# Products of constants that nobody reads, in TensorE's waits from the last logits to the first gate product

## The reference

```python
def _hmoe(x, w_rg, b_rg, w_re, b_re, w1, w3, w2):
    xt = x.reshape(B * T, D)
    lg = (xt @ w_rg + b_rg)                       # 4 groups
    g = jnp.argmax(lg, axis=-1)
    le = (xt @ w_re + b_re).reshape(-1, 4, 4)     # 4 experts in each group
    le_g = jnp.take_along_axis(le, g[:, None, None], axis=1)[:, 0]
    top_v, top_i = lax.top_k(le_g, 2)
    wts = softmax(top_v) * softmax(lg)[g]
    gate = ...                                    # 16 wide, two entries a row
    a = jnp.einsum('nd,edf->nef', xt, w1)         # gate products
    u = jnp.einsum('nd,edf->nef', xt, w3)         # up products
    hdn = jax.nn.silu(a) * u * gate[..., None]
    return jnp.einsum('nef,efd->nd', hdn, w2)     # down products
```

## Time and profile before

| | |
|---|---|
| runs of the kernel before | 1141.06, 1141.35, 1142.93 us; median 1141.35 us |
| profiled execution | span 1140.6 us; the page gives no other time for it |
| TensorE busy | 1031.9 us, 90% |
| VectorE, ScalarE, GpSimd busy | 544.0, 274.0, 211.2 us |
| chain that ended last | TensorE 83%, DMA 8%, VectorE 5% |
| moved by DMA | 150.10 MB, mean 132 GB/s |

### The profile page before, as it was taken

One profiled execution on the slowest core, in us unless ns is written; L12 is line 12 of the kernel. 1 busy time (PEld: TensorE's weight loads), 2 busy tenths in 40 slices (PEclk: granted clock), 3 DMA queues, 4 the chain that ended last, 5 costly groups with the idle time before them and its releaser, 6 DMA issues.

```text
span 1140.6 us, 17296 instructions
## 1 busy us (share of the span) xinstructions
PE 1031.9 (90%) x6808; PEld 615.6 (54%) x6808; DVE 544.0 (48%) x987; ACT 274.0 (24%) x557; POOL 211.2 (19%) x202
## 2 busy tenths in 40 slices
PE   7999999979999987999999999983589989899856
PEld 4666666645656544665666666552345454455322
DVE  1541033354555547577765866746234333332137
ACT  1552112221222223333333333220111111111113
POOL 0000000000111123345534533400100000000056
PEclk9999999989999989999999999995699999899978
DMA  9120202020000064101001001159399986957756
GB/s 379 60 74 1 74 1 74 1 78 1 1 0 1 1 222 174 47 20 37 20 19 37 20 19 37 48 195 422 113 363 355 331 312 208 372 193 235 256 207 258
DMA packets 30475, 150.10 MB, mean 132 GB/s; under 512 B 5602, under 2 KB 6050, under 8 KB 21322
## 3 DMA queue, kind: packets, MB, share of 16 engines
q1 hardware_dynamic: 24730, 125.96, 29.9%
q0 software_dynamic: 5248, 18.94, 4.8%
q10 hardware_dynamic: 432, 4.35, 1.0%
HBM read 317.31 MB, written 23.82 MB: 299 GB/s over the span
## 4 chain that ended last, share of the span: by engine, by line
PE 83%; DMA 8%; DVE 5%; issue 2%; SPq 1%; ACT 0%; POOL 0%; DVEq 0%; POOLq 0%; ACTq 0%
PE psum L1712 18%; PE psum L779 10%; PE psum L1763 10%; PE psum L792 8%; PE psum L1385 5%; PE psum L1351 5%; PE psum L1374 4%; PE psum L820 4%; DMA x_cm<-in_w_up 3%; PE psum L1397 2%; PE psum L1730 1%; DMA hg_q<-in_w_down 1%; PE psum L754 1%; PE psum L1336 1%; DMA weight_slots<-in_w_gate 1%
## 5 line engine op out<-in xcount | busy, mean ns | idle before, releaser
L1712 PE MATMUL psum<-x_cm,weight_slots 128*128 128x344 f32 x720 | 209.0, 453 | 0.0
L1712 PEld LDWEIGHTS psum<-x_cm,weight_slots 128*128 128x128 f32 x720 | 136.6, 190 | 71.9 <-issue 1.1
L1763 PE MATMUL psum<-weight_slots,x_cm 128*128 128x512 f32 x256 | 113.6, 597 | 0.0
L1351 PE MATMUL psum<-conv_qk,scratch 128*32 128x512 f32 x320 | 75.7, 617 | 10.8 <-issue 7.2
L1374 PE MATMUL psum<-weight_slots,scratch 128*32 128x256 f32 x1280 | 77.4, 396 | 8.1 <-DMA weight_slots<-in_w_gate 4.3
L1385 PE MATMUL psum<-conv_qk,scratch 128*32 128x256 f32 x640 | 74.3, 386 | 5.5 <-DMA x_cm<-in_w_up 5.4
L1763 PEld LDWEIGHTS psum<-weight_slots,x_cm 128*128 128x128 f32 x256 | 47.9, 192 | 54.2 <-issue 54.2
L1351 PE MATMUL psum<-hg_q,scratch 128*32 128x512 f32 x320 | 75.7, 617 | 0.0
L1385 PE MATMUL psum<-hg_decay,scratch 128*32 128x256 f32 x320 | 74.1, 386 | 0.0
L1385 PE MATMUL psum<-x_cm,scratch 128*32 128x256 f32 x320 | 74.1, 386 | 0.0
L820 PEld LDWEIGHTS psum<-scratch 128*128 128x128 f32 x448 | 58.7, 194 | 24.4 <-issue 22.7
(11 more groups left out here) (388 smaller groups left out, 1649.4 us busy)
## 6 DMA issues: line engine op xcount, KB each, us to landing
weight_slots<-in_w_gate SPq DMA_DIRECT2D x80, 1024.0 KB
conv_qk<-in_w_up SPq DMA_DIRECT2D x40, 1024.0 KB
conv_qk<-in_w_down SPq DMA_DIRECT2D x40, 1024.0 KB
hg_q<-in_w_down SPq DMA_DIRECT2D x40, 1024.0 KB
hg_decay<-in_w_up SPq DMA_DIRECT2D x20, 1024.0 KB
x_cm<-in_w_up SPq DMA_DIRECT2D x20, 1024.0 KB
weight_slots<-in_w_in SPq DMA_DIRECT2D x6, 2048.0 KB, 8.2
y_slots<-scratch SPq DMA_DIRECT2D x10, 512.0 KB, 8.5
```

The source lines that it names most:

```text
L1351: m = mm(PS[lane, 5 + half, :], hidT[:, k, lane], w_down[q][:, k, half * 512:(half + 1) * 512], start=(k == 0), stop=(k == 1))
L1712: i = mm(PS[0:m, idx % 4, 0:PIECE], lhs_of(k), xT[:, k, n * PIECE:(n + 1) * PIECE], start=(k == 0), stop=(k == KD - 1))
L1763: i = mm(PS[:, bank, :], xT[:, k, c * P:(c + 1) * P], w_slot(g)[:, k, :], start=(k == 0), stop=(k == KD - 1))
```

## The change

A helper `fill(n)` issues n products of the identity with the first 512 columns of the constants, into bank 3. It is called eight times with 34 products in all. Nothing reads bank 3 between there and the up products, which begin with `start=True` and overwrite it. No wait is added or removed. Nothing else of the program changes, but lines behind the helper have moved: 745 to 750, 754 to 759, 896 and 897 to 905 and 906, 1322 to 1332, 1326 to 1337, 1336 to 1347, 1374 to 1387; the fills are line 741.

```diff
--- before.py
+++ after.py
@@ -735,6 +735,11 @@
         pe.wait_ge(s.hg_k_ready, H)
         pe.wait_ge(s.hq_silu, H)
 
+        def fill(n):
+
+            for _ in range(n):
+                mm(PS[:, 3, :], ident, cst[:, 0:512], start=True, stop=True)
+
         def turn_x1(c):
 
             r = x_rows(c)
@@ -888,14 +893,18 @@
         pe.wait_ge(s.hgs_ready, NCH)
         route(NCH - 3)
         turn_x1(NCH - 2)
+        fill(1)
         route(NCH - 2)
+        fill(2)
         turn_x1(NCH - 1)
+        fill(2)
         route(NCH - 1)
+        fill(8)
 
         pe.wait_ge(s.esum_ready, 1)
         mm(PS[:, 6, 0:NTT * NE], const("before"), esum.rearrange("p e i -> p (e i)"), start=True, stop=True)
         mm(PS[:, 7, 0:NTT * NE], ones, esum.rearrange("p e i -> p (e i)"), start=True, stop=True).then_inc(s.ranked, 1)
-        tensor_moe(pe)
+        tensor_moe(pe, fill)
 
     def scalar_rest(act, link, tell):
         A = nc.scalar.activation
@@ -1316,10 +1325,12 @@
             out_dma(sp, t["out_y"][c * P:c * P + r], pair_of[c][0:r, 0])
         sp.wait_ge(s.outputs, 16 * outs[0])
 
-    def tensor_moe(pe):
+    def tensor_moe(pe, fill):
         mm = nc.tensor.matmul
+        fill(2)
         pe.wait_ge(s.tile_column, 2)
         mm(PS[0:1, 5, 0:TILES], tile_col, ident[:, 0:TILES], start=True, stop=True).then_inc(s.tile_row, 1)
+        fill(12)
         pe.wait_ge(s.onehots, 1)
         for q in range(2 * NTT):
             half = 64 * (q % 2)
@@ -1351,7 +1362,9 @@
                         m = mm(PS[lane, 5 + half, :], hidT[:, k, lane], w_down[q][:, k, half * 512:(half + 1) * 512], start=(k == 0), stop=(k == 1))
             m.then_inc(s.down_done, 1)
 
+        fill(6)
         turn_x(0, 0)
+        fill(1)
 
         def turn_hid(n):
 
```

## The result

The change makes the kernel faster. In 18 runs of each, the median went from 1143.23 to 1135.93 us; the ratio of the changed kernel to the one before is 0.9922, with a 95% interval of 0.9905 to 0.994, so 0.6 to 0.95% are won. The medians lie 7.3 us apart (a ratio of 0.9936); 0.9922 of 1143.23 would be 8.9 us. The forecast was 7.6 of 1141.35 us, a ratio of 0.9933. The profiled execution of the changed kernel took 1135.78 us, with a span of 1133.9: 1.9 us of a run lie outside its span.

The account below looks back on a forecast made before the run. TensorE, busy 90%, was taken as the bound, its real products from 769 to 820 mostly at half clock; gains of 7.98 less 0.35 gave 7.6 us off 1141.35, so 1133.7, range 1131.2 to 1138.4.

Parts of the forecast that it names:

- last transposes: Transposes ahead of the last router products: from 1.94 to 1.06 us at the full clock, 0.88 gained.
- last router products: Router products of the last row chunk: from 3.60 to 1.86 us at the full clock, 1.74 gained.
- slot products: Products of line 1326 before the gather: 4.07 us, about half at the full clock, 2.0 gained (ends 1.0 and 2.1).
- gather transposes: Transposes of the first gather: from 1.97 to 1.06 us at the full clock, 0.91 gained.
- first gate products: Gate products of the first tile: from 5.51 to 3.66 us at the full clock, 1.85 gained.
- The late start of 0.35: Two fills behind the last transposes: 1.72 us in a wait of 1.36, so 0.35 us late.
- The count products: Lines 896 and 897: from 1.33 us to an assumed 0.73 at the full clock, 0.6 gained (ends 0.3 and 0.7).
- "Hidden" groups: Groups of fills shorter than their waits, costing nothing, such as 8 fills of 6.9 us in 7.48, 12 of 10.3 in 11.64.
- The first rival: Clock falls at 768.5 all the same and fills bring it back: net gain 4.1 us, 1137.3; chance 0.24.
- The loop: Stretch from 820 to 1087, where the clock falls in four places, 1.9 us each; allowed plus or minus 2.5 us.
- the second rival: Four more clock falls in the loop cancel the gain: 1141.3; chance 0.10, shared with a hold-up elsewhere.
- The slower rival: Fills never win the clock, cost 1.72 us each and stand in the way: 27 us, 1168.6; chance 0.04.

Follow-up runs that it names:

- the tail: The changed kernel with 15 more fills behind the last down products, in the wait for the gather of the results; ratio to the kernel before 0.992.
- one fill for two: The changed kernel with one fill in place of two on either side of the last transposes, plus 15 fills behind the last down products; ratio to the kernel before 0.9938.

## Why the prediction was right

- **The clock held from the first fill on, and the products were cut as the rows said.** The forecast per term and what it measured, in us: last transposes 0.88 and 0.90; last router products 1.74 and 1.74; the counts 2.28 nearer in all for 2.27 forecast; slot products 2.0 and 1.90; gather transposes 0.91 and 0.82; first gate products 1.85 and 1.85.
- **The late start of 0.35** lay elsewhere than forecast, and it is luck that the sum is the same. The pair ahead of the last transposes was put at nothing, because VectorE would not have let them start sooner; the one behind at 0.35. Measured, the transposes start 0.17 us later than in the kernel before (8.25 us from the common start for 8.08), and the pair behind them costs the other 0.18. Without the pairs the transposes start at 7.83: 0.25 us were there to be had, which the prediction had ruled out.
- **The count products** were bounded at 0.3 to 0.7 and taken at 0.6. From the start of 905 to the end of 906 it is 0.76 us (784.01 to 784.36 + 0.41), for 1.33: 0.57.
- **The sum.** The first gate products start 5.17 us nearer to the common start and take 1.85 less: 7.0 us, 7.6 forecast. The missing 0.6 is in four pieces: 0.19 in VectorE's run between the counts and the slot products (14.47 us before, 14.66 now), 0.23 in the wait for the gather (6.10 from the end of the sums' turn to its transposes, 6.33 now; in the second profile of the changed kernel it was 6.13, so this piece is no cost of the change), 0.10 and 0.09 in the slot and gather terms above. The span is 6.7 us shorter (1140.6 to 1133.9). From the end of the first gate products to the end of the span 318.8 us pass before and 318.9 now, within the 2 us of the prediction; in the second profile it was 322.6, outside them. That the first pair of profiles agrees so well is luck in part: both lost the same 17 us at half clock in the loop.
- **Where it came out.** 1135.93 for 1133.7: of the 2.2 us, 1.9 are the base. The median of the kernel before was 1141.35 in three runs and 1143.23 in eighteen. The gain of 7.6 lies between the 7.3 us of the medians and the 8.9 of the ratio.
- **"Hidden" groups** were hidden: 0.52 and 1.27 us idle are left, where the prediction said 0.6 and 1.2. The 12 fills for 8 show that the 0.52 is all the room there is.
- **The first rival** was priced rightly, and was not what happened. What the prediction had from the Trainium skill (TensorE: Matmul & The Clock Gate, "Part 4: PE-mode transpose") in its favour, that transposes would not count, is refuted for these fp32 transposes by the run with fills as transposes. Nor had the clock fallen right behind the transposes in the kernel before: it fell at 768.9, 2.0 us after their end and 0.6 us into the router products. What made the difference in that stretch was one fill of 0.86 us: without it 3.35 us are lost.
- **The loop.** I allowed 2.5 us either way. From the start of the first gate products to the end of the last down products the changed kernel took 269.9 us in one profile and 273.4 in the other, the kernel with the last five groups, whose loop is the same code, 263.9, and the one without the first fill 276.2. So the loop varies by twelve microseconds from one execution to the next, which is as much as the runs spread. My 2.5 us rested on four slow groups in one profile, and was too small for a single run. Most of this is the clock, as the windows of the shortest and the longest of the four loops show (the clock is the third column from the end):

```profile
813.85:1077.78 263.93, 239.82 (x3393) 127.42 (x3392) 87.58 (x145) 42.11 (x61) 16.86 (x18) 0.99 0.81 289
813.28:1089.52 276.24, 250.43 (x3393) 130.68 (x3392) 87.61 (x145) 42.18 (x61) 16.89 (x18) 0.95 0.77 276
```

  By windows of 0.5 us the clock was at half for 17, 20, 3 and 27 us of the four loops, in the order above. Half of what the others have more than the third is 7, 8.5 and 12 us, and they are 6.0, 9.5 and 12.3 us longer. It is not all: the loop of the kernel with the tail, again the same code, took 274.3 us with 14 at half clock. So the second rival does act in single runs, in both directions; what starts a fall in one execution and not in the next stays open.
- **The slower rival** (fills never win the clock) did not come about with products of 512 columns; with 20 columns it did.

## What to carry to other kernels

Where a serial hand-over between engines leaves TensorE idle by a few microseconds at a time, look at the granted clock of the real products behind each wait; filling the waits with products that nobody reads bought 7 us for 29 us of extra work, in a kernel whose TensorE was already 90% busy. Size each group by the idle time in the timeline: in the wait of 7.5 us, 8 products hid and 12 made the next product 2.8 us late (2.2 at the first gate products), and in the one of 11.6 us, 6 were too few to keep the clock. A group that is slightly too long (0.35 us) can still be right, if a shorter one loses the clock, and what the fills are made of matters: products of 128x512 and transposes of 128x128 held the clock, products of 20 columns did not, and no width between was tried. In a loop where most steps do not wait, fills may cost more than they bring: here the clock was at 1.00 throughout and the kernel was not faster. And where the time left goes with the clock lost elsewhere, as in this loop, single runs can't rank versions.

## What the runs showed of the hardware

- In 69 us whose fills were products of 20 columns, TensorE was busy for 68 and its weight loads for 67, and the granted clock stayed at 0.50 for all of it. TensorE's busy share alone did not tell its clock.
- Eight transposes of 128x128 held the clock as one product of 512 columns did, at the same time (0.88 us for 0.86).
- An idle stretch of 2.30 us behind four fills left the clock at 1.00; one of 6.41 us behind six did not.
- The clock can fall while TensorE is at work and not only in a wait: at 775.5, near the end of the last router products, with one fill for two; at 773.3, near the end of the last transposes, without the pairs.
- The same loop code took 263.9 to 276.2 us in four executions, with 3 to 27 us of it at half clock.
